# Attention kernel on one core: the slope-times-distance term of the latent heads added by TensorE behind each score matmul

## The chip, the cores and the metric

One core of one Trainium2 chip runs the whole program. The metric is the device time of one execution in microseconds. Three runs of the kernel before gave 2083.8, 2086.52 and 2086.84 us; the median is 2086.52 us.

## The reference, cut to what matters

The reference is three transformer layers for one sequence of 512 tokens at width 1024. Only the last layer's attention is touched here. It has 16 heads of dimension 64. Heads 0 to 7 of the kernel's order ("dilated" heads) use three causal windows; heads 8 to 15 ("latent" heads) attend to at most 128 keys that an indexer chose:

```
s = einsum('bqhr,bqkr->bhqk', q_lat, c_sel) * HEAD_DIM ** -0.5
dist = t_pos - idx                        # how far back the key lies
s = s - slopes[h] * dist
s = where(idx <= t_pos, s, -inf)
p = softmax(s)
```

The slopes of the latent heads are 2^-1 to 2^-8. The kernel computes all keys on and below the block diagonal and adds a large negative number where the indexer did not choose a key.

## The kernel before, in words

**Stages.** TensorE (PE) walks through 302 weight chunks (13 projections and feed-forward stages) with three one-pass matmuls per tile (lines L421 to L423: both operands split into a high and a low part in the rounded format fp32r). GpSimd splits the weights (L403, L405), SyncE's queue loads them. Between `attn_in` and `attn_out` lies the attention of the last layer, which is the part at issue.

**The attention in pairs.** Sixteen heads are done in eight pairs p = 0 to 7; pairs 0 to 3 are the dilated heads, pairs 4 to 7 the latent ones. Head a = 0 of a pair has its 64 query and key dimensions on partitions 0 to 63 of the tile `T2`, head a = 1 on partitions 64 to 127. The 512 queries are four blocks j = 0 to 3 of 128, and block j needs keys 0 to 128(j+1), so a head has 128 + 256 + 384 + 512 = 1280 score columns.

**PE's order** (written out by hand). `scores(p)` makes eight plain float32 matmuls (L863), one for each head and block in the order `SCORE_ORDER`, which alternates the heads: (0,3), (1,3), (0,1), (1,2), (0,2), (1,1), (0,0), (1,0). A float32 matmul leaves two records in the trace (two passes over its columns). The two heads' results lie in different banks but for (0,1) and (1,1), which share one: (1,1) waits for the semaphore `att_half` that (0,1) raises. `turn(p, pieces)` transposes the probabilities (L882), `values(p)` multiplies them with the values (L896). PE's loop over p is: turn(p, pieces 0 and 1); scores(p+2); turn(p, pieces 2, 3 and 4); values(p). `scores(p+2)` waits for `att_z` of both heads of pair p+1, that is, until VectorE has read their scores from PSUM.

**VectorE's order.** `bias(g)` for head g makes what is to be added to the scores. For g < 8 it is one instruction (L1453, 128x512). For g >= 8 it is four (L1457), one for each block: distance (`DL`) times minus the slope plus the indexer's mask (`SC`), into `BI`. `logits(g)` (L1470, four instructions) adds `BI` to the scores in PSUM, writes the result to SBUF and takes the row maximum; L1474 negates the maxima. `normalise(g)` (L1479, L1481) divides by the row sums. `pair_low(k)` (L1486) makes the low part of a pair's output. The loop over p is: bias(2p+4), bias(2p+5), pair_low(p-1), normalise(2p+2), logits(2p+4), normalise(2p+3), logits(2p+5). From p = 2 the two bias calls are those of latent heads; the last ones are at p = 5.

**ScalarE's order.** `exps(2p+2)` (L1847: exponential with row sums, each with a record that reads the sum), `copy_turned(p)` (four copies L1859 and one L1861, each behind a piece of `turn`), `exps(2p+3)`, `pair_high(p)` (L1867).

**Small loads.** Before the stage `idx_in`, when PE has ended the chunks before it, ScalarE issues four DMAs (L1786 to L1789: the index weights, the distances, two small projections), then computes the square root of a norm (`root`, L1794). VectorE waits for their semaphore `small_loaded` before it splits the index weights (L1393, L1395), which PE needs behind the sixth chunk of `idx_in` (its matmuls stand as `mix<-h_hi,b_wihi`).

Of the kernel before, what the change touches and what calls it, by code (L numbers as in the profile page):

```python
# [26 lines left out]
F32 = mybir.dt.float32  # L27
F32R = mybir.dt.float32r
U8 = mybir.dt.uint8
ALU = mybir.AluOpType  # L30
# [3 lines left out]
P = 128  # L34
D = 1024
T = 512
KT = D // P
NTB = T // P
# [6 lines left out]
TRI = sum(T - P * i for i in range(NTB))  # L45
# [48 lines left out]
SLOPE_A, SLOPE_B = slopes()  # L94
# [69 lines left out]
        self.n = self.base + count * per  # L164


def build(nc, x_in, wstream, adastream, c_in, cols_in, const_in, mask_in, gatew_in, wiw_in, wuk_in, wuv_in, out):
    with ExitStack() as ctx:
        def sem(name):
            return ctx.enter_context(nc.semaphore(name))  # L170
# [1 line left out]
        def sb(name, shape, dt=F32, where=ctx):  # L172
            return where.enter_context(nc.sbuf_tensor(name, shape, dt))
# [85 lines left out]
        with ExitStack() as r:  # L259
            sb("b_over_h", [P, 2 * KT * T], F32, r)  # L260

            T2 = sb("b_t2", [P, 18, T], F32, r)
            VA = sb("b_va", [P, NTB, T], F32, r)
            SC = sb("b_score", [P, TRI], F32, r)
            DL = sb("b_dist", [P, 1024], F32, r)
            BI = sb("b_bias", [P, 4, TRI], F32, r)
            zmem = ada_raw[:].rearrange("p s n -> p (s n)")
            Z = [zmem[:, TRI * i:TRI * i + TRI] for i in range(3)] + [cact[:].rearrange("p m n -> p (m n)")[:, 0:TRI]]  # L270
            PS = sb("b_pt", [P, 2, TRI], F32, r)
            VB = work
            SB5 = M + [G[3]]
            wuk = sb("b_wuk", [P, 4, P], F32, r)
            wuv = sb("b_wuv", [P, T], F32, r)
            wi_f = BI[:, 0, 0:64]
            wi_hi = sb("b_wihi", [P, 64], F32R, r)
            wi_lo = sb("b_wilo", [P, 64], F32R, r)
            wi = sb("b_wi", [P, 32], F32, r)
            wirow = PS[0:8, 0, 0:T]  # L280
            top8 = sb("b_top8", [P, 24], F32, r)
            mx = sb("b_mx", [P, 16], F32, r)
            nmx = sb("b_nmx", [P, 16], F32, r)
            rsm = sb("b_rsm", [P, 16], F32, r)
            sm = sb("b_sm", [P, 16], F32, r)
# [38 lines left out]
        def sig(name):  # L324

            if name not in S:
                S[name] = sem(name)
            return S[name]
# [90 lines left out]
        def _(pe):  # L419
# [206 lines left out]
            for h in range(4):  # L626
# [3 lines left out]
                o = M[h]  # L630
# [218 lines left out]
            def scores(p):  # L849
                if p == 0:  # L850
                    pe.wait_ge(sig("vb_copied"), 4)
                    pe.wait_ge(gfree[3], G0["attn_out"][3])
                else:
                    if p == 4:
                        pe.wait_ge(gfree[1], G0["attn_out"][1])
                    pe.wait_ge(sig("att_z"), 2 * p)
                q0, k0 = (10, 14) if p < 4 else (6, 0)
                for a, j in SCORE_ORDER:
                    rows = slice(64 * a, 64 * a + 64)
                    b, o = PAIR_J[a][j]  # L860
                    if (a, j) == (1, 1):
                        pe.wait_ge(sig("att_half"), p + 1)
                    mm = pe.matmul(SB5[b][:, o:o + P * (j + 1)], T2[rows, q0 + p % 4, j * P:(j + 1) * P],  # L863
                                   T2[rows, k0 + p % 4, 0:P * (j + 1)], start=True, stop=True)
                    if (a, j) == (0, 1):
                        mm.then_inc(sig("att_half"), 1)
                    if j == 0:
                        mm.then_inc(sig(f"att_s{a}"), 1)
# [52 lines left out]
        def _(dve):  # L921
# [467 lines left out]
            norm(7, 6, col("g_attn", 0, 8), (96, 104), first_gain=col("final_g", 0, 8))  # L1389
            normed_x(4, col("final_g", 0, 8), bank=M[1], done=True)  # L1390

            dve.wait_ge(small_loaded, 112)
            dve.tensor_copy(wi_hi[:], wi_f[:]).then_inc(sig("wi_hi"), 1)  # L1393
            dve.wait_ge(sig("wi_hi"), 1)
            dve.tensor_tensor(wi_lo[:], wi_f[:], wi_hi[:].bitcast(F32), ALU.subtract).then_inc(sig("wi_split"), 1)  # L1395
# [1 line left out]
            def seg(j, n=None):  # L1397
                return slice(OFF_J[j], OFF_J[j] + (P * (j + 1) if n is None else n))
# [51 lines left out]
            def bias(g):  # L1450

                if g < 8:
                    dve.scalar_tensor_tensor(out=BI[:, g % 4, 0:T], in0=DL[:, 0:T], scalar=-SLOPE_A[g], in1=DL[:, T:2 * T],  # L1453
                                             op0=ALU.mult, op1=ALU.add).then_inc(sig("att_b"), 1)
                else:
                    for j in range(NTB):
                        ins = dve.scalar_tensor_tensor(out=BI[:, g % 4, seg(j)], in0=DL[:, 384 - P * j:T], scalar=-SLOPE_B[g - 8],  # L1457
                                                       in1=SC[:, seg(j)], op0=ALU.mult, op1=ALU.add)
                    ins.then_inc(sig("att_b"), 1)

            def logits(g):
                q = 4 * (g % 4)
                dve.wait_ge(sig(f"att_s{g % 2}"), g // 2 + 1)
                dve.wait_ge(sig("att_b"), g + 1)
                if g >= 4:
                    dve.wait_ge(sig("att_t"), 5 * (g // 2 - 2) + 5)
                for j in range(NTB):
                    b, o = PAIR_J[g % 2][j]
                    bi = BI[:, g % 4, 384 - P * j:T] if g < 8 else BI[:, g % 4, seg(j)]
                    ins = dve.tensor_tensor_reduce(Z[g % 4][:, seg(j)], SB5[b][:, o:o + P * (j + 1)], bi, 1.0, TAKEN, ALU.add, ALU.max,  # L1470
                                                   mx[:, q + j:q + j + 1])
                ins.then_inc(sig("att_z"), 1)
                dve.wait_ge(sig("att_z"), g + 1)
                dve.tensor_scalar(nmx[:, q:q + 4], mx[:, q:q + 4], -1.0, None, ALU.mult).then_inc(sig("att_m"), 1)  # L1474
# [19 lines left out]
            logits(2)  # L1494
            logits(3)
            for p in range(8):
                if p + 2 < 8:
                    bias(2 * p + 4)
                    bias(2 * p + 5)
                if p >= 1:  # L1500
                    pair_low(p - 1)
                for a in range(2):
                    if p + 1 < 8:
                        normalise(2 * p + 2 + a)
                    if p + 2 < 8:
                        logits(2 * p + 4 + a)
# [10 lines left out]
        def _(act):  # L1517
# [269 lines left out]
            act.dma_start(DL[:], const_in[:, CST["dist"]:CST["dist"] + 1024]).then_inc(small_loaded, 16)  # L1787
            act.dma_start(wuk[:], wuk_in).then_inc(small_loaded, 16)
            act.dma_start(wuv[:], wuv_in).then_inc(small_loaded, 16)  # L1789

            def root():
                nrm[0] += 1
# [121 lines left out]
def prepare(i):  # L1914
# [35 lines left out]
    cols[0:8, COL["gate_b"] + 1] = i["odd_gate_b"][0, 8:16]  # L1950
    c, m = constants()

    def small(w_):
        n = w_.shape[1]
        return np.ascontiguousarray(w_.reshape(8, 128, n).transpose(1, 0, 2).reshape(128, 8 * n))
# [3 lines left out]
    return {  # L1959
        "x_in": np.ascontiguousarray(i["x"][0].T.reshape(8, 128, 512).transpose(1, 0, 2)),  # L1960
        "wstream": wstream, "adastream": adastream, "c_in": np.ascontiguousarray(np.broadcast_to(crow, (128, 2, 1024))), "cols_in": cols, "const_in": c, "mask_in": m,
        "gatew_in": small(gates), "wiw_in": small(wi),
        "wuk_in": np.ascontiguousarray(i["w_uk_2"][0].reshape(4, 128, 128).transpose(2, 0, 1)),
        "wuv_in": np.ascontiguousarray(i["w_uv_2"][0].transpose(1, 0, 2).reshape(128, 512)),
    }
# [13 lines left out]
```

## Time and profile before

| what | us |
|---|---|
| median of three runs | 2086.52 |
| the profiled execution, its own time | 2092.76 |
| its span from first to last instruction | 2090.7 |
| PE busy in the span | 1973.9 |
| VectorE (DVE) busy | 1072.5 |
| ScalarE (ACT) busy | 448.9 |
| GpSimd (POOL) busy | 1197.3 |
| mean granted TensorE clock | 0.969 |

The profiled execution is one run; its own time lies 6.2 us above the median of the three. The span leaves out 2.1 us of that execution's time, which lie before its first and behind its last instruction. A busy time counts only instructions that do work; waits are not counted. PE's ends are modelled: successive PE records overlap, so that the distance between two starts says more than a duration.

### The profile page before, as it was taken

The numbers are of one execution on the slowest core, as the hardware profiler recorded it, in microseconds if no ns is written. First come the engines' busy times: TensorE is split into PE (matmuls) and PEld (weight loads), VectorE is DVE, ScalarE is ACT, GpSimd is POOL, SyncE is SP. The second block draws the span as 40 slices with busy tenths as digits, with TensorE's granted clock in tenths as the row PEclk, the third lists the DMA queues.
The fourth block names the chain that finished last, engine by engine and source line by source line (L and its number), as shares of the span: only waits on it lengthen the run. The fifth ranks groups of instructions, "written<-read, shape, count | busy, mean of one in ns | idle before, by whom it ended". The sixth has DMA issues, their size and how long they took to land.

```text
span 2090.7 us, 25307 instructions
## 1 busy us (share of the span) xinstructions
PE 1973.9 (94%) x8738; PEld 1580.3 (76%) x8738; DVE 1072.5 (51%) x1631; ACT 448.9 (21%) x773; POOL 1197.3 (57%) x907
## 2 busy tenths in 40 slices
PE   6997887999999999998999999999998799999998
PEld 5786764888888887764788888887776588888886
DVE  4557633665554734456676555223876663223222
ACT  3300033221111013143121111002225621111100
POOL 2674500578887775522567888774352056666673
PEclk7998988999999999999999999999999999999999
DMA  7443200355554532211245554332121022222232
GB/s 288 170 142 121 98 4 0 101 181 190 192 200 171 210 128 81 80 47 34 86 158 199 188 193 161 108 108 87 51 71 41 1 81 91 100 94 97 101 106 75
DMA packets 67516, 242.22 MB, mean 116 GB/s; under 512 B 7642, under 2 KB 8026, under 8 KB 67458
## 3 DMA queue, kind: packets, MB, share of 16 engines
q1 hardware_dynamic: 64448, 232.81, 31.7%
q10 hardware_dynamic: 3010, 8.60, 1.1%
q8 instruction: 41, 0.67, 0.1%
q14 instruction: 17, 0.14, 0.0%
HBM read 239.28 MB, written 2.10 MB: 115 GB/s over the span
## 4 chain that ended last, share of the span: by engine, by line
PE 87%; DVE 5%; ACT 3%; DMA 2%; issue 2%; POOL 1%; SPq 0%; DVEq 0%; ACTq 0%; POOLq 0%
PE gemm L421 23%; PE gemm L423 23%; PE gemm L422 23%; DMA w_raw<-wstream 2%; PE gemm L448 1%; PE gemm L450 1%; PE gemm L449 1%; PE mix L603 1%; PE mix L421 1%; PE mix L422 1%; PE gemm L710 1%; PE mix L423 1%; PE mix L505 1%; PE gemm L724 1%; PE mix L863 1%
## 5 line engine op out<-in xcount | busy, mean ns | idle before, releaser
L405 POOL TENSOR_TENSOR w_lo<-w_raw,w_hi 128x1024 fp32r<-128x1024 f32 x302 | 748.2, 2478 | 25.2
L421 PE MATMUL gemm<-h_hi,w_hi 128*128 128x512 f32 x1616 | 635.0, 393 | 15.4 <-DVE h_lo L1030 6.0
L423 PE MATMUL gemm<-h_hi,w_lo 128*128 128x512 f32 x1616 | 631.4, 391 | 0.0
L422 PE MATMUL gemm<-h_lo,w_hi 128*128 128x512 f32 x1616 | 631.2, 391 | 0.0
L402 POOL TENSOR_TENSOR pool_gate<-pool_gate 128x1 f32<-128x1 f32 x298 | 119.4, 401 | 820.2 <-PE gemm L423 667.0
L421 PEld LDWEIGHTS gemm<-h_hi,w_hi 128*128 128x128 f32 x1616 | 305.2, 189 | 85.9 <-issue 16.1
L422 PEld LDWEIGHTS gemm<-h_lo,w_hi 128*128 128x128 f32 x1616 | 305.1, 189 | 63.5 <-issue 0.5
L423 PEld LDWEIGHTS gemm<-h_hi,w_lo 128*128 128x128 f32 x1616 | 304.7, 189 | 63.8
L403 POOL TENSOR_SCALAR w_hi<-w_raw 128x1024 fp32r<-128x1024 f32 x302 | 342.1, 1133 | 18.8 <-DMA w_raw<-wstream 18.8
L927 DVE CUSTOM_DVE_ANT_0 ada_raw<-ada_raw,c_act 128x1024 f32<-128x1024 f32 x128 | 210.4, 1654 | 168.7 <-DMA ada_raw<-adastream 168.5
L423 PE MATMUL gemm<-p_hi,w_lo 128*128 128x512 f32 x528 | 205.4, 389 | 0.0
L421 PE MATMUL gemm<-p_hi,w_hi 128*128 128x512 f32 x528 | 205.4, 389 | 0.0
L422 PE MATMUL gemm<-p_lo,w_hi 128*128 128x512 f32 x528 | 205.4, 389 | 0.0
L945 DVE SCALAR_TENSOR_TENSOR x_res<-gemm,modv,x_res 128x512 f32<-128x512 f32 x48 | 35.9, 748 | 248.8 <-PE gemm L423 248.8
L1215 DVE TENSOR_TENSOR work<-work,gemm 128x512 f32<-128x512 f32 x66 | 45.4, 688 | 176.7 <-PE gemm L423 138.9
L1523 ACT ACTIVATE sq_tile<-x_res 128x512 f32 (+1 forms) x56 | 35.2, 631 | 442.0 <-DVE x_res L945 435.1
L1217 DVE TENSOR_TENSOR p_lo<-work,p_hi 128x512 f32 x66 | 95.7, 1449 | 61.4 <-ACT p_hi L1694 61.4
L1187 DVE TENSOR_TENSOR sq_acc<-sq_acc,sq_tile 128x512 f32<-128x512 f32 x42 | 99.1, 2360 | 36.7 <-ACT sq_tile L1523 36.7
L421 PEld LDWEIGHTS gemm<-p_hi,w_hi 128*128 128x128 f32 x528 | 99.1, 188 | 20.7
L422 PEld LDWEIGHTS gemm<-p_lo,w_hi 128*128 128x128 f32 x528 | 99.1, 188 | 20.6
L423 PEld LDWEIGHTS gemm<-p_hi,w_lo 128*128 128x128 f32 x528 | 99.1, 188 | 20.4
L1688 ACT ACTIVATE work<-work 128x512 f32<-128x512 f32 x44 | 27.8, 633 | 310.4 <-DVE work L1210 310.4
(310 smaller groups left out, 2070.6 us busy)
## 6 DMA issues: line engine op xcount, KB each, us to landing
w_raw<-wstream SPq DMA_DIRECT2D x302, 512.0 KB, 3.5
ada_raw<-adastream SPq DMA_DIRECT2D x128, 512.0 KB, 4.6
a_early<-adastream SPq DMA_DIRECT2D x4, 1024.0 KB, 13.4
a_early<-adastream ACTq DMA_DIRECT2D x4, 1024.0 KB, 23.2
out<-x_res SPq DMA_DIRECT2D x8, 256.0 KB, 2.2
x_res<-x_in SPq DMA_DIRECT2D x2, 512.0 KB, 6.4
c_act<-c_in ACTq DMA_DIRECT2D x2, 512.0 KB, 15.0
x_res<-x_in ACTq DMA_DIRECT2D x2, 512.0 KB, 9.3
```

The lines of the kernel that those rows point to most:

```text
L402: pool.tensor_tensor(pgate[:], pgate[:], pgate[:], ALU.mult)
L403: pool.tensor_scalar(whi[s][:], raw[:, u % RAW, :], 1.0, 0.0, ALU.mult, ALU.add).then_inc(w_hi_done, 1)
L405: pool.tensor_tensor(wlo[s][:], raw[:, u % RAW, :], whi[s][:].bitcast(F32), ALU.subtract).then_inc(w_split, 1)
L421: pe.matmul(out_ap, w_h, r_h, start=first, stop=False)
L422: pe.matmul(out_ap, w_h, r_l, start=False, stop=False)
L423: return pe.matmul(out_ap, w_l, r_h, start=False, stop=last)
L927: dve.tensor_tensor_reduce(w, w, c, 1.0, start, ALU.mult, ALU.add, total).then_inc(ada_used, 1)
L945: dve.scalar_tensor_tensor(out=X[:, ds(m, 1), :].rearrange("p a t -> p (a t)"), in0=G[bank][:], scalar=modv[:, ds(gate + m, 1)], in1=X[:, ...
L1187: dve.tensor_tensor(sqacc[:], sqacc[:], sqt[:, m % 2, :], ALU.add).then_inc(sq_added, 1)
L1215: dve.tensor_tensor(work[:, 2 + jj, :], y, G[2 * jj + 1][:], ALU.mult).then_inc(gfree[2 * jj + 1], 1)
L1217: dve.tensor_tensor(Plo[:, ds(2 * i + jj, 1), :].rearrange("p a t -> p (a t)"), work[:, 2 + jj, :], Phi[:, ds(2 * i + jj, 1), :].rearrange ...
L1523: act.activation(sqt[:, slot, :], X[:, ds(m, 1), :].rearrange("p a t -> p (a t)"), ACT.Square).then_inc(sq_ready, 1)
```

## The change

Two constant rows for each head replace the product of slope and distance on VectorE. For query t and key s, minus slope times (t - s) is the sum of 1 times (slope * s) and t times (-slope), which is a matmul with a contraction over two rows. `SLP` holds (slope * s) and (-slope) on rows 0 and 1 of each head's 64 partitions, `QROW` holds 1 and t, and the other 62 rows are zero. Behind each score matmul of the pairs 4 to 7, PE adds their product to the same PSUM columns, in fp32r, with the same 64 partitions and the same width. VectorE makes no bias for heads 8 to 15 any more; `logits` adds the mask `SC` itself. Two DMAs (1 MB and 256 KB) bring the rows into `VA` and `T2[:, 17]`, which are not yet in use then, and two VectorE copies round them into `SLP` and `QROW`.

```diff
-            BI = sb("b_bias", [P, 4, TRI], F32, r)
+            BI = sb("b_bias", [P, 4, T], F32, r)
+            SLP = sb("b_slopes", [P, 4, T], F32R, r)
+            QROW = sb("b_qrow", [P, T], F32R, r)
...
             def scores(p):
                 if p == 0:
                     pe.wait_ge(sig("vb_copied"), 4)
+                    pe.wait_ge(sig("slopes_ready"), 2)
...
                     mm = pe.matmul(SB5[b][:, o:o + P * (j + 1)], T2[rows, q0 + p % 4, j * P:(j + 1) * P],
-                                   T2[rows, k0 + p % 4, 0:P * (j + 1)], start=True, stop=True)
+                                   T2[rows, k0 + p % 4, 0:P * (j + 1)], start=True, stop=p < 4)
+                    if p >= 4:
+                        mm = pe.matmul(SB5[b][:, o:o + P * (j + 1)], QROW[rows, j * P:(j + 1) * P], SLP[rows, p - 4, 0:P * (j + 1)],
+                                       start=False, stop=True)
                     if (a, j) == (0, 1):
                         mm.then_inc(sig("att_half"), 1)
...
-            dve.wait_ge(small_loaded, 112)
+            dve.wait_ge(small_loaded, 144)
+            dve.tensor_copy(SLP[:], VA[:]).then_inc(sig("slopes_ready"), 1)
+            dve.tensor_copy(QROW[:], T2[:, 17, :]).then_inc(sig("slopes_ready"), 1)
             dve.tensor_copy(wi_hi[:], wi_f[:]).then_inc(sig("wi_hi"), 1)
...
-                else:
-                    for j in range(NTB):
-                        ins = dve.scalar_tensor_tensor(out=BI[:, g % 4, seg(j)], in0=DL[:, 384 - P * j:T], scalar=-SLOPE_B[g - 8],
-                                                       in1=SC[:, seg(j)], op0=ALU.mult, op1=ALU.add)
-                    ins.then_inc(sig("att_b"), 1)
...
-                dve.wait_ge(sig("att_b"), g + 1)
+                if g < 8:
+                    dve.wait_ge(sig("att_b"), g + 1)
...
-                    bi = BI[:, g % 4, 384 - P * j:T] if g < 8 else BI[:, g % 4, seg(j)]
+                    bi = BI[:, g % 4, 384 - P * j:T] if g < 8 else SC[:, seg(j)]
...
             for p in range(8):
-                if p + 2 < 8:
+                if p < 2:
                     bias(2 * p + 4)
                     bias(2 * p + 5)
...
             act.dma_start(wuv[:], wuv_in).then_inc(small_loaded, 16)
+            act.dma_start(VA[:].rearrange("p a t -> p (a t)"), slope_in[:, 0:2048]).then_inc(small_loaded, 16)
+            act.dma_start(T2[:, 17, :], slope_in[:, 2048:2560]).then_inc(small_loaded, 16)
```

## Rows read from the trace of the kernel before

**Rows 1.** The page, parts 1 and 4: busy time, and the chain that ended last.
```profile
PE 1973.9 (94%) x8738; PEld 1580.3 (76%) x8738; DVE 1072.5 (51%) x1631; ACT 448.9 (21%) x773; POOL 1197.3 (57%) x907
...
PE 87%; DVE 5%; ACT 3%; DMA 2%; issue 2%; POOL 1%; SPq 0%; DVEq 0%; ACTq 0%; POOLq 0%
```

**Rows 2.** Windows, one per pair's turn: PE, PEld, DVE, ACT, POOL busy; clock; DMA.
```profile
1596.67:1607.31 10.64, 7.58 (x53) 5.19 (x53) 8.42 (x33) 7.68 (x24) 0.00 (x0) 1.00 0.00 0
1607.31:1619.29 11.98, 9.10 (x53) 6.62 (x53) 10.33 (x38) 7.54 (x23) 0.00 (x0) 0.86 0.01 2
1619.29:1629.84 10.55, 7.58 (x53) 5.16 (x53) 10.23 (x38) 7.59 (x24) 0.00 (x0) 1.00 0.00 0
1654.80:1666.10 11.30, 9.79 (x52) 5.46 (x52) 2.14 (x6) 5.42 (x14) 0.00 (x0) 0.78 0.01 2
```

**Rows 3.** Line L1457 alone: its instructions, least, median and longest in ns.
```profile
L1457 DVE SCALAR_TENSOR_TENSOR b_bias<-b_dist,b_score x32: 280/483/684, 1607.3 to 1643.1; 128x128 f32<-128x128 f32 x8, 128x256 f32<-128x256 f32 x8, 128x384 f32<-128x384 f32 x8, 128x512 f32<-128x512 f32 x8
```

**Rows 4.** Timeline of DVE, a turn of dilated, then one of latent heads.
```profile
1601.37 0.29 DVE L1470 CUSTOM_DVE_ANT_0 ada_raw<-mix,b_bias 128x128 f32<-128x128 f32 x1 [1.36 <-PE gemm L882]
...
1619.35 3.29 DVE L1457 SCALAR_TENSOR_TENSOR b_bias<-b_dist,b_score 128x128 f32<-128x128 f32 x8
...
1624.55 0.28 DVE L1470 CUSTOM_DVE_ANT_0 ada_raw<-mix,b_bias 128x128 f32<-128x128 f32 x1
...
1626.65 0.18 DVE L1479 RECIPROCAL b_rsm<-b_sm 128x4 f32<-128x4 f32 x1 [0.17 <-ACT ada_raw L1847]
```

**Rows 5.** The chain of waits in the latent turn: start, us, what.
```profile
1621.82 0.60 PE gemm L882 x4
...
1623.85 0.60 ACT b_pt L1861
1624.44 2.19 ACT ada_raw L1847 x8
...
1627.07 1.07 DVE ada_raw L1481 x3
...
1629.84 0.69 PE mix L863
```

**Rows 6.** Windows around two scores() calls, line L863 alone: PE and PEld busy, clock.
```profile
1607.31:1610.74 3.43, 3.43 (x16) 2.67 (x16) 0.67 0.00 0
1619.29:1621.75 2.46, 2.46 (x16) 1.76 (x16) 1.00 0.00 0
```

**Rows 7.** Timeline of PE: one pair's scores seen 0.4 and 0.9 us in; one indexer head.
```profile
1596.67 0.70 PE L863 MATMUL mix<-b_t 64*128 64x512 f32 x2 [1.84 <-DVE b_mx L1470]
...
1596.67 1.13 PE L863 MATMUL mix<-b_t 64*128 64x512 f32 x4 [1.84 <-DVE b_mx L1470]
...
1459.36 2.42 PE L813 MATMUL gemm<-b_t 64*128 64x128 f32 x8
```

**Rows 8.** The chain of waits: a one-pass matmul of 512 columns behind a float32 one.
```profile
1502.53 0.86 PE mix L531 x2
1503.38 0.23 PE gemm L421
```

**Rows 9.** The page, part 6, and ACT's timeline: DMAs issued ahead of `idx_in`.
```profile
a_early<-adastream ACTq DMA_DIRECT2D x4, 1024.0 KB, 23.2
...
1409.82 0.46 ACTq L1789 DMA_DIRECT2D b_wuv<-wuv_in  x1
1412.29 0.26 ACT L1794 ACTIVATE rms<-mix,cols 128x4 f32<-128x4 f32 x1 [3.08 <-PE mix L510]
```

**Rows 10.** Timelines of DVE and PE in `idx_in`, and DVE's line L1481.
```profile
1437.44 0.62 DVE L1393 CAST b_wihi<-b_bias 128x64 fp32r<-128x64 f32 x1
...
1463.72 1.27 DVE L1409 TENSOR_SCALAR b_score<-ada_raw,b_wi 128x128 f32<-128x128 f32 x4 [25.41 <-ACT ada_raw L1819]
...
1453.74 0.39 PE L421 MATMUL mix<-h_hi,b_wihi 128*8 128x512 f32 x1
...
L1481 DVE TENSOR_SCALAR ada_raw<-ada_raw,b_rsm 128x512 f32<-128x512 f32 x8 | 3.8, 480 | 0.0
```

More of the change, by code:

```diff
@@ L164, in left, with build @@
         self.n = self.base + count * per
-def build(nc, x_in, wstream, adastream, c_in, cols_in, const_in, mask_in, gatew_in, wiw_in, wuk_in, wuv_in, out):
+def build(nc, x_in, wstream, adastream, c_in, cols_in, const_in, mask_in, gatew_in, wiw_in, wuk_in, wuv_in, slope_in, out):
     with ExitStack() as ctx:
@@ L1951, in prepare @@
     c, m = constants()
+    rows = np.zeros((128, 5, 512), np.float32)
+    for h in range(8):
+        rows[64 * (h % 2), h // 2], rows[64 * (h % 2) + 1, h // 2] = SLOPE_B[h] * np.arange(512), -SLOPE_B[h]
+    rows[[0, 64], 4], rows[[1, 65], 4] = 1.0, np.arange(512)
     def small(w_):
@@ L1961, in prepare @@
         "wstream": wstream, "adastream": adastream, "c_in": np.ascontiguousarray(np.broadcast_to(crow, (128, 2, 1024))), "cols_in": cols, "const_in": c, "mask_in": m,
-        "gatew_in": small(gates), "wiw_in": small(wi),
+        "slope_in": rows.reshape(128, 2560), "gatew_in": small(gates), "wiw_in": small(wi),
         "wuk_in": np.ascontiguousarray(i["w_uk_2"][0].reshape(4, 128, 128).transpose(2, 0, 1)),
```

## The prediction

> **What bounds the kernel now.** I read the page first: PE is busy 1973.9 of 2090.7 us and carries 87% of the chain that ended last [rows 1]. So anything given to PE must be asked for its price, and anything taken from DVE for what it released. The change touches the turns of the latent pairs, and there the average says little: I cut the attention into one window per turn, from one start of scores() to the next [rows 2]. The dilated turn takes 10.64 us with DVE busy 8.42, the latent one 10.55 us with DVE busy 10.23. DVE looks like the bound of the latent turn, but the dilated turn, with 1.8 us less of DVE work, is no shorter. That is the first sign that DVE only fills a gap that another chain leaves.
>
> The timelines say which. In the latent turn, which starts at 1619.29, DVE makes the biases (3.29 us), then pair_low and normalise, and starts logits at 1624.55, 5.26 us into the turn, without idling. In the dilated turn it has idled 1.36 us before the same step, for the transposes on PE, and starts it 4.70 us into the turn. In both it must then wait for ScalarE's exponentials; in the latent turn for 0.17 us, at 1626.65 [rows 4, 5]. The chain of waits of the latent turn passes through none of the bias: transposes behind the scores (1621.82), the last copy (1623.85), the exponentials (2.19 us), normalise and logits of the second head, and the next scores at 1629.84 [rows 5]. So the turn is: scores on PE (2.46 us [rows 6]), then 8.1 us of transposes, copies, exponentials, normalise and logits, one behind the other. The scores stand at full length in this chain, because PE issues the transposes behind them.
>
> **The change part by part.**
>
> Removed: 32 bias instructions on DVE, 8 in each of four turns [rows 3], 3.29 us a turn, 13.2 us in all [rows 4]. I cost this at nothing. What hides it is the chain PE, ScalarE. Without it DVE comes to logits 3.29 us earlier and must wait there until the transposes end, 4.70 us into the turn as in the dilated one; logits starts 0.56 us earlier than now, and then normalise still waits for the exponentials, which end where they end. The bound from above is 3.29 us a turn, if the wait of 0.17 us were an illusion of the records; it is nearest to zero, since two turns with such different DVE work differ by 0.09 us. Reading the mask in place of the bias is the same shape and costs the same.
>
> Added on PE: eight one-pass matmuls behind the eight score matmuls of a pair, four pairs. A one-pass matmul of 512 columns takes 0.23 us from start to start, also right behind a float32 one, so changing the format costs nothing visible [rows 8]. One head has 1280 columns: 1280/512 x 0.23 = 0.575 us. Do the two heads of a pair share this time? Now they do: 0.4 us into a pair's scores two records of 512 columns have started, 0.9 us in it is four, and a pair ends in 2.46 us where one indexer head, the same 1280 float32 columns on one half of the rows, takes 2.42 us [rows 6, 7]. The heads run side by side, each on its 64 rows, though the code lists both passes of one head's matmul before those of the other. The added matmuls have the same rows and widths and alternate in the same way, so I take 0.575 us a pair. The ends are 0 (they fill pauses, of which 2.46 us for 2.42 us leaves few) and 1.15 us (the added ones of the two heads don't overlap); the row nearest is that of the score matmuls themselves.
>
> The first of the four, scores(4), now takes 3.43 us because the granted clock there is 0.67 on average, part of it at 1.2 GHz [rows 6]. Up to its start nothing changes, so I expect the low clock in the same place, and its added matmuls at twice the time: 1.15 us. Sum on PE's chain: 3 x 0.575 + 1.15 = 2.9 us. After the last pair's scores the same delay runs on to attn_out, since values and transposes of the pair wait behind them.
>
> The semaphore att_half is now raised behind the added matmul of (0,1). Behind the waiting (1,1) stand (0,0) and (1,0) of the same pair and all transposes. But head 1 has its own added matmuls of 512 and 384 columns before it, and these are longer than head 0's of 512 and 256, so the wait grows by nothing.
>
> The Trainium skill, page "TensorE: Matmul & The Clock Gate", section "What overlaps and what doesn't", speaks against that: matmuls start and end in program order, "strict FIFO, no reordering". By that rule a head's matmul could not begin before the first head's last pass has begun, and each added matmul would move it further back; the trace of before disagrees already, as four records have started after 0.9 us.
>
> Ahead of idx_in: two more DMA issues on ScalarE's queue. The four that stand there take 0.33 to 0.63 us each, the last starts at 1409.82; two more of 0.5 us end near 1411.3, and root, next in the queue, waits for PE until 1412.29 in any case [rows 9]. Cost nothing, with 1 us to spare; if they took over 1 us each, what is more would go to the norm and so to the chain. The 1.25 MB must have landed when DVE comes to the split of the index weights at 1437.44. The large DMAs on this queue at the kernel's start landed in 23.2 us with three others of their size under way [rows 9], which gives 1434. The copies: 2048 + 512 columns, between 0.48 us (L1481) and 0.62 us (the cast at 1437.44) for each 512, so 2.4 to 3.1 us. The split would end near 1441.5, PE needs it at 1453.74 and DVE's next work comes at 1463.72 after 25.41 us of idling [rows 10]. Hidden with 12 us to spare; SyncE's and GpSimd's queues are not passed. The new wait of scores(0) for slopes_ready has long been met.
>
> **Sum.** 0 on DVE + 2.9 on PE + 0 ahead of idx_in. The profiled execution would go from 2092.8 to 2095.7 us. It is 6.2 us above the median of the runs shown, so I put the sum on the median: 2086.5 + 2.9 = 2089.4 us. That is 0.14%, less than the 0.2% (4.2 us) that a measurement of this kernel can tell from no change.
>
> **The rivals.**
>
> *The second head waits.* PE must hold the added matmul of head 0, behind two passes, before it can start head 1. If what it can hold is one matmul less than that, the heads run one after the other. A pair's scores then last at least 2 x 2.42 = 4.84 us with the added ones beside the other head's passes, at most 4.84 + 1.15 = 5.99 us. Against 2.46 us now that is 2.4 to 3.5 us for each of four pairs, 9.5 to 14.1 us; I take 11.5: 2098.0 us. Slower is decided from 1 us a pair on. For it: the trace shows overlap for alternating matmuls alone, not for two of a head in a row. Against it: the overlap reaches over two passes already. Partly so, with 5 to 8 us, belongs here.
>
> *DVE was the bound.* If logits of the first head, 0.56 us earlier, moves ScalarE's exponentials of the next turn and these the copies, the latent turns shrink. At the most each loses its 3.29 us and gains 0.575 us: 4 x 2.7 = 10.9 us, 2075.6 us. For it: DVE is busy 10.23 of 10.55 us. Against it: the dilated turn, and PE and ScalarE with 7.6 us busy in a fixed order [rows 2].
>
> *The clock.* The turn at 1607.31 has 0.86 of the clock and lasts 1.43 us longer than its neighbours; the stretch from 1654.80 has 0.78, which on 11.30 us is some 2.5 us [rows 2]. PE works more in these turns and may be granted more: without both lows the sum is 2.9 - 0.6 - 1.4 - 2.5 = -1.6, 2084.9 us. Or the shifted work meets one low more: 1.4 to 2.5 us, 2091.4 us at the middle.
>
> *It doesn't do what it says*: the biases are removed beyond doubt; only the load ahead of idx_in could undo it, if it lands after 1449 or so; then each further us costs one.
>
> **How the numbers follow.** Forecast, its own range 2087.5 to 2091.5: 0.60. The second head waits, wholly or partly: 0.16. The clock, better 0.08, worse 0.10. DVE was the bound: 0.04. The late load: 0.02. The range starts at 2084.9, rounded to 2084.5 (better clock), and ends at 2097.0, which takes in the upper bound of the added matmuls (5.75 us), the worse clock and the lower half of the waiting head, and leaves out its upper half and the gain on DVE. Faster by over 0.2% (below 2082.3): the 0.04. Slower by over 0.2% (above 2090.7): 0.16 + 0.06 of the clock + 0.02 + 0.04 of the forecast's upper edge = 0.28. Within: 0.68.
>
> **What would show it.** Right: scores of pairs 5 to 7 last 3.0 us in place of 2.46, the turns 11.1 us, and DVE idles some 3 us more in each, most of it before logits for the transposes. Wrong: the scores records of a pair stretched to 4.8 us or more, with four 512-column records no longer started within 0.9 us (the second head waits); turns shorter than 10.5 us (DVE was the bound); ScalarE's root starting behind 1412.3, or PE idle before the index weights (the loads).

## The result, and the profile after

The changed kernel took 2092.11 us (median of 19 runs, 2089.19 to 2098.14), the kernel before 2087.84 us (median of 19 runs beside them). The ratio is 1.0024, with a 95% interval of 1.0017 to 1.0031, that is 3.5 to 6.5 us more. The time lies in the wide range given (2084.5 to 2097.0), but 0.6 us above the forecast's own range of 2087.5 to 2091.5. The ratio is a little over the 0.2% that I had set as the bound of "no change" (a chance of 0.28), and its interval reaches from just under that bound to 0.31%. It reaches 0.07% to either side, so that such a comparison tells more than the 0.2% I had thought.

The page of the changed kernel answers to [rows 1]. PE's busy time is as before, and so is its share of the chain (87%); VectorE has 6.9 us less to do over the whole program.

```profile
PE 1974.2 (94%) x8770; PEld 1581.5 (76%) x8770; DVE 1065.6 (51%) x1601; ACT 448.9 (21%) x773; POOL 1197.6 (57%) x907
```

A stretch that can be compared runs from the first score matmul of pair 3 to the first matmul of `attn_out`. Everything behind it takes 424.6 us in both profiles, and ahead of it the executions differ by several us from one to the next, change or none. I call it the stretch. The windows answer to [rows 2]: first the whole stretch, before and after, then the turns of the changed kernel. (PE, PEld, DVE, ACT, POOL busy; then the granted clock.)

```profile
1596.67:1666.10 69.43, 51.40 (x324) 34.30 (x324) 53.69 (x192) 46.17 (x130) 0.00 (x0) 0.93 0.00 1
```

```profile
1592.37:1665.47 73.10, 55.01 (x356) 37.89 (x356) 41.01 (x160) 46.12 (x130) 0.00 (x0) 0.91 0.00 1
...
1592.37:1603.00 10.63, 7.57 (x52) 5.18 (x53) 8.40 (x33) 7.67 (x24) 0.00 (x0) 1.00 0.00 0
1603.00:1615.64 12.64, 9.67 (x61) 7.34 (x61) 7.03 (x30) 7.50 (x23) 0.00 (x0) 0.86 0.01 2
1615.64:1626.70 11.06, 8.10 (x60) 5.73 (x60) 7.11 (x30) 7.57 (x23) 0.00 (x0) 1.00 0.00 0
1626.70:1637.78 11.08, 8.11 (x61) 5.75 (x61) 7.12 (x30) 7.60 (x24) 0.00 (x0) 1.00 0.01 1
1637.78:1665.47 27.69, 21.55 (x124) 13.89 (x124) 11.35 (x42) 15.77 (x41) 0.00 (x0) 0.82 0.00 1
```

The stretch grew from 69.43 to 73.10 us. VectorE's work in it fell from 53.69 to 41.01 us, and no turn became shorter for it. The last dilated turn is unchanged at 10.63 us. The latent ones stand at 12.64, 11.06 and 11.08 us against 11.98, 10.55 and 10.55 [rows 2], and from the last pair's scores to `attn_out` it is 27.69 us, where before it was:

```profile
1640.38:1666.10 25.72, 19.56 (x116) 12.18 (x116) 14.48 (x50) 15.78 (x42) 0.00 (x0) 0.87 0.01 2
```

So 0.66 + 0.51 + 0.53 + 1.97 = 3.67 us. The windows around the four scores() calls answer to [rows 6]; the clock is the number behind the bracketed counts and times.

```profile
1603.00:1607.46 4.46, 4.46 (x24) 3.85 (x25) 2.01 (x7) 0.87 (x2) 0.00 (x0) 0.64 0.00 0
1615.64:1618.62 2.98, 2.98 (x24) 2.34 (x24) 2.10 (x7) 0.96 (x2) 0.00 (x0) 1.00 0.00 0
...
1637.78:1642.39 4.61, 4.61 (x25) 3.65 (x25) 2.09 (x7) 0.96 (x2) 0.00 (x0) 0.63 0.00 0
```

At full clock the scores of a pair went from 2.46 to 2.98 us. The first and the last call had the low clock (0.64 and 0.63 on average). The first one did before, too [rows 6]; the last one did not.

PE's timeline of the second latent pair, seen 1.0 us in, answers to [rows 7], and VectorE's of that turn to [rows 4]:

```profile
1615.64 1.13 PE L866 MATMUL mix<-b_t 64*128 64x512 f32 x4 [1.85 <-DVE b_mx L1474]
1616.20 0.80 PE L869 MATMUL mix<-b_slopes,b_qrow 64*128 64x512 f32 x2
```

```profile
1620.83 0.29 DVE L1474 CUSTOM_DVE_ANT_0 ada_raw<-mix,b_score 128x128 f32<-128x128 f32 x1 [3.06 <-PE gemm L888]
...
1623.52 0.18 DVE L1483 RECIPROCAL b_rsm<-b_sm 128x4 f32<-128x4 f32 x1 [0.75 <-ACT ada_raw L1853]
```

Four score records and both added ones (L869) are there within 0.9 us: the heads still run side by side. VectorE is ready for logits 2.1 us into the turn, 3.1 us earlier than before, and idles 3.06 us until the transposes (L888) and later 0.75 us until the exponentials. The 3.29 us of [rows 4] became 3.6 us more of waiting (3.06 + 0.75 in place of 0.17). The chain of waits has the added matmuls in it and is otherwise that of [rows 5]:

```profile
1616.77 0.23 PE mix L869 x2
...
1618.69 0.60 PE gemm L888 x4
...
1621.32 2.18 ACT ada_raw L1853 x8
...
1623.94 1.07 DVE ada_raw L1485 x3
...
1626.70 0.69 PE mix L866
```

Ahead of `idx_in`, against [rows 9, 10]: ScalarE's timeline, then VectorE's and PE's.

```profile
1406.41 0.45 ACTq L1795 DMA_DIRECT2D b_t<-slope_in  x1
1407.96 0.26 ACT L1800 ACTIVATE rms<-mix,cols 128x4 f32<-128x4 f32 x1 [3.03 <-PE mix L512]
```

```profile
1433.16 1.65 DVE L1399 CAST b_slopes<-b_va 128x2048 fp32r<-128x2048 f32 x1
1434.73 0.41 DVE L1400 CAST b_qrow<-b_t 128x512 fp32r<-128x512 f32 x1
...
1459.44 1.27 DVE L1417 TENSOR_SCALAR b_score<-ada_raw,b_wi 128x128 f32<-128x128 f32 x4 [23.17 <-ACT ada_raw L1825]
```

```profile
1449.46 0.39 PE L423 MATMUL mix<-h_hi,b_wihi 128*8 128x512 f32 x1
```

The two new DMAs are issued by 1406.86 (the line shows the second of them), 1.1 us before root. VectorE made the copies in 1.65 + 0.41 us without waiting for the data and idled 23.17 us afterwards. From root to the index weights' first matmul it is 41.50 us, 41.45 before [rows 9, 10].

### The profile page after: what moved, and what is told of

It is laid out like the page before. It is cut to its first block, busy times and chain, and to the rows that moved or that the text cites. A ratio compares the mean times of both kernels' runs of the same rounds, so it can differ in the third digit from the quotient of the medians.

```text
span 2090.1 us, 25343 instructions
## 1 busy us (share of the span) xinstructions
PE 1974.2 (94%) x8770; PEld 1581.5 (76%) x8770; DVE 1065.6 (51%) x1601; ACT 448.9 (21%) x773; POOL 1197.6 (57%) x907
## 4 chain that ended last, share of the span: by engine, by line
PE 87%; DVE 5%; ACT 3%; DMA 2%; issue 2%; POOL 1%; SPq 0%; DVEq 0%; ACTq 0%; POOLq 0%
PE gemm L423 23%; PE gemm L424 23%; PE gemm L425 23%; DMA w_raw<-wstream 2%; PE gemm L450 1%; PE gemm L452 1%; PE gemm L451 1%; PE mix L605 1%; PE mix L423 1%; PE mix L424 1%; PE gemm L712 1%; PE mix L425 1%; PE mix L507 1%; PE mix L866 1%; PE gemm L726 1%
## 5 line engine op out<-in xcount | busy, mean ns | idle before, releaser
L933 DVE CUSTOM_DVE_ANT_0 ada_raw<-ada_raw,c_act 128x1024 f32<-128x1024 f32 x128 | 216.1, 1699 | 163.8 <-DMA ada_raw<-adastream 163.7
```

The source lines that it names most:

```text
L933: dve.tensor_tensor_reduce(w, w, c, 1.0, start, ALU.mult, ALU.add, total).then_inc(ada_used, 1)
```

## The experiments

Each kernel is compared with runs of the kernel before on the same chip. What it is written against (the changed kernel, or the one before) stands with it.

**1. No added matmuls** (changed kernel; the distance is added by nobody).

```diff
-                    if p >= 4:
-                        mm = pe.matmul(SB5[b][...], QROW[rows, ...], SLP[rows, p - 4, ...], start=False, stop=True)
```

> The changed kernel without the added matmuls: VectorE makes no bias for the latent heads and nobody adds the distance; the loads and the two copies ahead of idx_in stay. Measure: the stretch from the first score matmul of pair 3 to the first matmul of attn_out, 69.4 us before and 73.1 us after the change in the profiles. Theory (VectorE's bias work was wholly hidden, the added matmuls are the whole loss): scores of a latent pair 2.46 us again, the stretch 69.4 us or less by at most 0.2, time that of the kernel before (2087.8 us). Rival 1 (taking the bias away gave something back, and the added matmuls cost more than they show): the stretch is 66 us or less, the time 3 us or more below before. Rival 2 (the loads and copies ahead of idx_in cost something): time above before although the stretch is 69.4 us.

Measured: 2090.4 us, ratio to the kernel before 1.0002 (0.9991 to 1.0013). The stretch, and the scores of the second latent pair:

```profile
1597.51:1666.94 69.43, 51.36 (x325) 34.28 (x325) 41.02 (x160) 46.12 (x130) 0.00 (x0) 0.93 0.00 1
1620.18:1622.64 2.46, 2.46 (x16) 1.76 (x17) 2.10 (x7) 0.96 (x3) 0.00 (x0) 1.00 0.00 0
```

69.43 us to the hundredth, as in the kernel before, with 12.7 us less on VectorE. Rival 1 is out: taking the bias away gave nothing. Rival 2 is out as well, as loads and copies are in this kernel and the time is that of the kernel before.

**2. Added matmuls and biases both.** The 32 bias instructions are back on VectorE, into a tile that is read by nobody.

```diff
+                else:
+                    dve.wait_ge(sig("att_b"), g)
+                    for j in range(NTB):
+                        ins = dve.scalar_tensor_tensor(out=BX[:, seg(j)], in0=DL[:, 384 - P * j:T], scalar=-SLOPE_B[g - 8], in1=SC[:, seg(j)], ...)
+                    ins.then_inc(sig("att_b"), 1)
...
-                if p < 2:
+                if p + 2 < 8:
                     bias(2 * p + 4)
```

> The changed kernel with the added matmuls and also the 32 bias instructions on VectorE (their result is written and used by nobody, a wait on its own semaphore stands before each group). Theory: the bias work is hidden here as it was before; the latent turns last 11.1 us as after the change, the time is that of the changed kernel within 1 us (2092 us). With 0.17 us of VectorE's slack plus 0.52 us of longer scores it fits by 0.1 us or less, so up to 0.3 us a turn may show. Rival 1: each turn is 1 us or more longer than after the change, the time 2096 us or more.

Measured: 2096.46 us, ratio 1.0030 (1.0018 to 1.0042). The stretch and one turn:

```profile
1591.74:1664.79 73.05, 54.94 (x356) 38.15 (x356) 54.06 (x192) 46.11 (x130) 0.00 (x0) 0.91 0.00 1
1615.01:1626.08 11.07, 8.11 (x60) 5.74 (x61) 10.32 (x38) 7.58 (x24) 0.00 (x0) 1.00 0.00 0
```

73.05 us, and the turn of 11.07 us is that after the change, with VectorE busy 10.32 us in place of 7.11. The median lies 4 us above what I expected, and the rival had 2096 us or more; but on this chip the kernel before took 2089.51 us, the interval holds the changed kernel's ratio, and the rival's turns, 1 us longer each, are not there. The bias is hidden with the added matmuls as without.

**3. Each added matmul twice** (the distance counts double).

```diff
                     if p >= 4:
-                        mm = pe.matmul(...)
+                        for last in (False, True):
+                            mm = pe.matmul(..., start=False, stop=last)
```

> The changed kernel with each added matmul issued twice (the distance counts double). Theory: scores of a pair at full clock go from 2.46 (none) and 2.98 us (one) to 3.5 us, each turn 0.52 us longer than after the change, one of the four at the lower clock twice that; the stretch 73.1 + 2.6 = 75.7 us, the time 2.6 us above the changed kernel (2094.7 us). Rival (PE can hold one added matmul beside two passes but not two, so the second head waits): scores of a pair 4.8 us or more, the time 7 us or more above the changed kernel. Rival 2 (the clock took much of the loss by chance): the stretch moves by anything from 1 to 5 us, by where the low clock falls.

Measured: 2095.19 us, ratio 1.0029 (1.0017 to 1.0040). The stretch, and the scores of a pair that ran at full clock:

```profile
1593.00:1668.87 75.87, 58.06 (x389) 41.85 (x389) 40.92 (x160) 46.25 (x130) 0.00 (x0) 0.91 0.00 1
1630.39:1634.06 3.67, 3.67 (x32) 3.02 (x32) 2.10 (x7) 0.97 (x3) 0.00 (x0) 1.00 0.00 0
```

At full clock the scores take 3.67 us: the first added matmul of each block cost a pair 0.52 us, the second 0.69. The heads still overlap. That the stretch of 75.87 us meets the 75.7 of the theory is in part luck, as the second rival of the expectation would have it: the granted clock was 0.68 in the scores of pairs 4, 5 and 7, one pair more than after the change, and from the last pair's scores on it is 26.72 us at a clock of 0.87, where it was 27.69 us at 0.82. The times (ratio 1.0029 against 1.0024) are too coarse to show the further 2.8 us, as their intervals overlap.

**4. The added matmuls behind piece 4 of turn.** They leave the scores() call and stand where PE waits 0.78 us for ScalarE's last copy.

```diff
                 turn(p, (2, 3, 4))
+                if 4 <= p + 2 < 8:
+                    distances(p + 2)      # the eight added matmuls, then att_s0 and att_s1
                 values(p)
```

> The changed kernel with the eight added matmuls moved from behind each score matmul to behind the transposes of piece 4, where PE waits 0.78 us for ScalarE's last copy. Theory (only their place in the chain costs time): scores of a latent pair 2.46 us, the turns 10.5 to 10.7 us, the stretch 69.4 us, the time that of the kernel before (2087.8 us) though VectorE makes no bias. Rival: VectorE's logits, which now wait for the added matmuls 5.2 us into the turn, come later than the exponentials and the turn grows by 0.3 us or more: stretch 70.6 us or more.

Measured: 2089.19 us, ratio 1.0002 (0.9994 to 1.0011).

```profile
1592.48:1661.90 69.42, 54.51 (x356) 37.15 (x356) 41.01 (x160) 46.18 (x130) 0.00 (x0) 0.93 0.00 1
```

In three banks two blocks lie side by side, and here both are started before anything is added, so that the score product of the block written first is missing from its sum. The Trainium skill, page "PSUM — Partial Sum Buffer", section "The four PSUM rules", says that a start flag clears the written marks of the whole bank and that the next matmul without one overwrites. No time here shows the marks. The following kernel leaves the flag out for the second block of a bank:

```diff
-                                   T2[rows, k0 + p % 4, 0:P * (j + 1)], start=True, stop=True)
+                                   T2[rows, k0 + p % 4, 0:P * (j + 1)], start=(a, j) not in ((0, 0), (1, 0), (1, 1)) or p < 4, ...)
```

> As the added matmuls behind the transposes of piece 4, but the second score matmul in a bank that holds two blocks doesn't start an accumulation, so that the added matmuls find what they add to. Theory: the same times as in that run, stretch 69.4 us, time that of the kernel before. Rival: a flag changes the time: stretch off by 0.3 us or more.

Measured: 2086.99 us, ratio 0.9994 (0.9985 to 1.0004). The stretch, and the second latent turn:

```profile
1589.64:1659.06 69.42, 54.53 (x356) 37.18 (x356) 41.03 (x160) 46.16 (x129) 0.00 (x0) 0.93 0.00 1
1612.24:1622.78 10.54, 8.35 (x60) 5.86 (x61) 7.12 (x30) 7.59 (x24) 0.00 (x0) 1.00 0.00 0
```

The same matmuls as after the change, the same work on VectorE, and the stretch is back at 69.42 us: what cost time was their place in the chain. The further low of the clock, which the last pair's scores met after the change, is gone with it. VectorE has 41.0 us to do in place of 53.7, and the time is that of the kernel before.

**5. The heads in runs of three** (changed kernel, all pairs).

```diff
-SCORE_ORDER = [(0, 3), (1, 3), (0, 1), (1, 2), (0, 2), (1, 1), (0, 0), (1, 0)]
+SCORE_ORDER = [(0, 1), (0, 3), (0, 2), (1, 1), (1, 3), (1, 2), (0, 0), (1, 0)]
```

> The changed kernel with another order of the score matmuls in all eight pairs: (0,1), (0,3), (0,2), (1,1), (1,3), (1,2), (0,0), (1,0), three of head 0 and then three of head 1, each latent one with its added matmul behind it. It asks how far PE looks past a head's waiting matmuls, which is what the rival of the prediction hung on. Theory (each head's rows have a queue of limited length, which was long enough for one float32 matmul and one added one, and the doubling of the added ones did not fill it): the second head starts late, when most of the first's three are through; scores of a dilated pair near 4.3 us, of a latent pair near 5.3 us, each turn longer by the difference: stretch 73.1 + 0.9 to 1.8 a dilated pair's turn, 2 a latent one's, some 83 us in all, time 12 us or more above the changed kernel. Rival (the queue is long): the heads run side by side, scores of a latent pair 3.0 to 3.3 us, stretch 73 to 75 us.

Measured: 2104.38 us, ratio 1.0072 (1.0058 to 1.0087). Windows of PE alone (busy; clock): scores of a dilated and of a latent pair, and the stretch. Then PE's timeline in short windows: two lines of the dilated scores, the others of the latent ones.

```profile
1584.66:1587.77 3.11, 3.11 (x18) 1.00 0.02 7
1607.12:1613.22 6.10, 6.10 (x25) 0.72 0.00 0
1595.84:1684.05 88.21, 71.10 (x356) 0.81 0.00 1
```

```profile
1584.66 0.70 PE L866 MATMUL mix<-b_t 64*128 64x256 f32 x2
...
1585.19 0.70 PE L866 MATMUL mix<-b_t 64*128 64x512 f32 x2
...
1607.12 0.67 PE L866 MATMUL mix<-b_t 64*128 64x256 f32 x2 [1.93 <-DVE b_mx L1474]
1607.44 0.47 PE L869 MATMUL mix<-b_slopes,b_qrow 64*128 64x256 f32 x1
...
1608.20 0.79 PE L869 MATMUL mix<-b_slopes,b_qrow 64*128 64x512 f32 x1
1608.61 0.48 PE L866 MATMUL mix<-b_t 64*128 64x256 f32 x1
```

I had overlooked a semaphore in this order. Head 1 now begins with (1,1), which waits for `att_half`, and that is raised by (0,1), the first matmul of head 0 (by its added one in a latent pair). In a dilated pair this wait explains the whole delay: (0,1) ends at 1585.36, and (1,1) starts at 1585.41, 0.05 us later (its first record is the second one of the line at 1585.19, which also holds the first pass of (0,3)), although the second pass of (0,3) and all of (0,2) stand ahead of it and have not started. The call lost 0.65 us (3.11 for 2.46 us). In a latent pair the added matmul of (0,1) ends at 1607.91, but (1,1) starts only at 1608.61, 1.49 us after head 0's first record and still at full clock. Of these, 0.79 us are the wait for the semaphore. The other 0.70 us are not: there head 1 does start late, behind three matmuls of head 0 with their added ones, as a limited queue would have it. That it is a queue is argued, not shown; an order of the same kind without the semaphore was not run.

The latent calls took 6.10 us in three pairs, at a clock of 0.72, and 8.24 us in the last at 0.52, so I can't say what they take at full clock. The stretch of 88.21 us is 5 us beyond my figure, and the clock (0.81 over it, 0.91 after the change) has a large part in that.

**6. Turn before scores.** In the first of two, the kernel before has all pieces of turn(p) ahead of scores(p+2); in the second, the changed kernel.

```diff
-                turn(p, (0, 1))
+                turn(p, (0, 1, 2, 3, 4))
                 if p + 2 < 8:
                     scores(p + 2)
-                turn(p, (2, 3, 4))
                 values(p)
```

> The kernel before (biases on VectorE) with PE's loop in another order: all five pieces of turn(p), then scores(p+2), then values(p). So the scores leave the chain transposes, copies, exponentials. Theory: with that chain shorter VectorE becomes the bound of the latent turns: it is busy 10.23 us in each, so they last 10.2 to 10.5 us, while the dilated turns shrink to 9 us or so. Stretch 67 to 69 us (69.4 now), time 1 to 3 us below the kernel before. Rival (ScalarE and the semaphores set 10.5 us in any order): stretch 69 us or more.

> The changed kernel with the same order of PE's loop. Theory: now the work that the change takes from VectorE counts: its latent turns hold 7 us of VectorE's and 7.6 us of ScalarE's work, and last 8.5 to 9.5 us; the stretch is 63 to 66 us, 3 us or more shorter than that of the kernel before in the same order, and the time 4 to 7 us below the kernel before. Rival (the added matmuls and the waits for the exponentials keep the turn): turns of 10.3 us or more, no better than the kernel before in the same order.

Measured: 2087.86 us, ratio 1.0001 (0.9993 to 1.0010), and 2092.17 us, ratio 1.0018 (1.0009 to 1.0026). For kernels in another order I take the longer stretch from the first score matmul of pair 1 to `attn_out`: 94.97 us before, 98.64 us after the change. The long stretch and a latent turn of each:

```profile
1566.57:1661.10 94.53, 73.39 (x450) 50.14 (x449) 64.97 (x239) 57.93 (x162) 10.71 (x9) 0.95 0.07 23
1607.30:1617.65 10.35, 7.55 (x54) 4.94 (x53) 10.21 (x38) 7.59 (x22) 0.00 (x0) 0.99 0.00 1
```

```profile
1568.28:1666.71 98.43, 77.01 (x482) 52.62 (x481) 52.31 (x207) 57.83 (x162) 10.73 (x9) 0.93 0.06 22
1632.39:1643.25 10.86, 8.06 (x62) 5.52 (x61) 7.02 (x29) 7.59 (x22) 0.00 (x0) 1.00 0.01 2
...
DVE ada_raw L1473 <- PE mix L869: 16.4, 4, 5.3
ACT h_hi L1872 <- PE gemm L902: 14.2, 5, 3.8
```

Both theories fell, and the turns are those of the rivals. In the first kernel the last dilated turn takes 10.32 us (I had 9) and the latent one 10.35, so that VectorE's 2 us more of work do not show. In the second the last dilated turn takes 10.33 us and the latent one 10.86 at full clock, with 3.2 us less on VectorE: taking the bias away gave nothing, and the added matmuls cost their 0.5 us again. VectorE waits 16.4 us for the scores and ScalarE 14.2 us for the values (the wait list of the second kernel): the scores now wait for the transposes, the values for the scores, and ScalarE's next exponentials stand behind the output of the values. One chain was exchanged for another of nearly the same length.

**7. The second head's exponentials early.** ScalarE waits 2.2 us for the transposes behind the scores, and the second head's exponentials take 2.18 us, are ready to run, and stand behind that wait. Three kernels move them ahead of it: the kernel before, the changed kernel, and the changed one with the added matmuls between pieces 3 and 4 of turn.

```diff
                 if p + 1 < 8:
                     exps(2 * p + 2)
-                copy_turned(p)
+                if p >= 1:
+                    pair_high(p - 1)
+                copy_turned(p, (0, 1))
                 if p + 1 < 8:
                     exps(2 * p + 3)
-                pair_high(p)
+                copy_turned(p, (2, 3, 4))
...
-                if p >= 1:
-                    pair_low(p - 1)
-                for a in range(2):
-                    if p + 1 < 8:
-                        normalise(2 * p + 2 + a)
-                    if p + 2 < 8:
-                        logits(2 * p + 4 + a)
+                normalise(2 * p + 2); pair_low(p - 1); normalise(2 * p + 3)
+                logits(2 * p + 4); logits(2 * p + 5)
```

> The kernel before with another order on ScalarE and VectorE. ScalarE: exps(2p+2), pair_high(p-1), two copies, exps(2p+3), three copies; so the second head's exponentials (2.18 us) run where ScalarE waited 2.2 us for the scores on PE, and leave the chain. VectorE: normalise of both heads, then logits of both. Measure here: from the first score matmul of pair 1 to the first matmul of attn_out, 95.0 us before, 98.6 us after the change. Theory (VectorE's bias was hidden only by that chain): once the chain is shorter the 3.29 us stand in the turn: VectorE's work of a latent turn adds up to 10.2 us and more, so the latent turns stay at 10.2 to 10.9 us, the dilated ones (1.3 us of bias) fall to 9.0 to 9.6 us. Stretch 91 to 95 us, time 0 to 4 us below the kernel before. Rival (PE and ScalarE set the turns in this order too): latent turns as short as dilated ones, 9.0 to 9.6 us, stretch 88 us or less.

> The changed kernel, added matmuls behind each score matmul, with that same order on ScalarE and VectorE. Theory: VectorE's latent turn is 3.3 us shorter and PE's scores 0.52 us longer; turns of 9.0 to 9.9 us, latent ones no longer than dilated ones by more than 0.6 us; stretch 88 to 91 us, shorter than that of the kernel before in the same order, time 5 to 8 us below the kernel before. Rival (the added matmuls cost as much as the bias there): latent turns 10.2 us or more.

> The same order, with the added matmuls between the transposes of pieces 3 and 4, where PE waits for ScalarE's copy. Theory: latent turns 9.0 to 9.5 us, 0.3 to 0.5 us shorter than with the added matmuls among the scores; stretch 86 to 89 us, time 6 to 10 us below the kernel before, faster than both kernels. Rival (they are no longer on the chain in this order): the same within 0.2 us a turn as with them among the scores.

Measured, in this order: 2085.74 us, ratio 0.9986 (0.9977 to 0.9995); 2083.34 us, ratio 0.9973 (0.9964 to 0.9983); 2082.14 us, ratio 0.9969 (0.9957 to 0.9981). The long stretch and latent turns of each:

```profile
1566.61:1659.17 92.56, 74.32 (x450) 50.44 (x449) 65.39 (x239) 56.88 (x162) 10.75 (x9) 0.93 0.07 23
1600.87:1611.86 10.99, 9.18 (x53) 5.82 (x52) 10.85 (x40) 8.11 (x25) 0.00 (x0) 0.84 0.01 2
1611.86:1621.37 9.51, 7.59 (x54) 5.16 (x53) 9.37 (x35) 6.63 (x21) 0.00 (x0) 1.00 0.00 0
```

```profile
1564.31:1653.11 88.80, 73.39 (x482) 51.62 (x481) 53.20 (x207) 56.87 (x162) 10.75 (x9) 0.96 0.07 24
1607.89:1617.22 9.33, 8.03 (x61) 5.73 (x60) 7.17 (x29) 7.49 (x23) 0.00 (x0) 1.00 0.00 0
```

```profile
1566.86:1655.63 88.77, 74.50 (x481) 52.09 (x480) 53.21 (x207) 56.86 (x162) 10.73 (x9) 0.96 0.07 24
1610.46:1619.79 9.33, 8.32 (x62) 5.87 (x61) 7.17 (x29) 7.49 (x23) 0.00 (x0) 1.00 0.00 0
```

Both changed kernels beat the kernel before and the change as it was made: 88.80 and 88.77 us in place of 94.97 and 98.64. Of the 6.2 us against the kernel before, 1.4 come with the clock: pair 4's turn, 11.98 us there, has no low in either. Their turns are 9.33 us whether the added matmuls are among the scores or not, so that in this order they are no longer on the chain (the rival of the last expectation, and my own figure of 0.3 to 0.5 us was wrong). The kernel before in the same order has VectorE busy 9.37 of 9.51 us in its turn at full clock: the bias is now the bound, but only by 0.18 us; I had expected 10.2 us or more. That its stretch of 92.56 us lies in my range of 91 to 95 is luck: some 3 of the 3.8 us by which it is longer than that of the changed kernel come with the clock (0.84 and 0.85 in two turns). What makes the clock fall there and not in the other two I have not shown, nor, then, how much of the 2.4 us between the medians the bias is worth.

**8. The changed kernel again.**

> The changed kernel once more, unchanged. In its profile one stretch of half clock (3.4 us) more than before lies in the last pair's scores; it took 1.5 of the 3.7 us by which the attention grew. Theory (the work sets where the clock falls, since the low 1.2 us into the scores of pair 4 came at the same place in every profile): it comes again, in the scores or transposes of one of the pairs 5 to 7, and the stretch from the first score matmul of pair 3 to attn_out is 72.8 to 73.4 us. Rival (a chance of that one execution): no further low, the stretch is 71.3 to 71.8 us.

Measured: 2093.58 us, ratio 1.0019 (1.0007 to 1.0031). The stretch, and the scores of pair 6:

```profile
1598.30:1671.36 73.06, 54.95 (x357) 38.16 (x357) 41.04 (x160) 46.10 (x129) 0.00 (x0) 0.91 0.00 1
1632.63:1636.92 4.29, 4.29 (x24) 3.65 (x24) 2.10 (x7) 0.97 (x3) 0.00 (x0) 0.67 0.00 0
```

73.06 us. The further low came again, this time in pair 6 instead of pair 7, at nearly the same price: pair 6's turn took 12.63 us, pair 5's 11.06.

## Why the prediction was right or wrong

**VectorE's bias, cost nothing: right, and shown.** With the biases and without, the stretch is 69.43 us if nothing is added on PE (experiment 1), and 73.05 and 73.10 us if it is (experiment 2). The cover that I named, the chain of PE and ScalarE, is what hides it: shortened by 1.2 us in experiment 7, it no longer quite does. The rival "DVE was the bound" is out.

**The added matmuls, 0.575 us a pair: right in kind, 0.52 us.** The two heads share the time. The rival "the second head waits" did not come about, and the doubling of experiment 3 did not bring it about; in experiment 5, with three matmuls of one head in a row, 0.70 us of such a wait show beside that for `att_half`. The rule of the Trainium skill that I set against it (page "TensorE: Matmul & The Clock Gate", section "What overlaps and what doesn't": matmuls start in the order of the program) does not hold in these traces. After the change head 0's added matmul stands ahead of head 1's score matmul in the program, and both score matmuls are under way 0.5 us before the first added one starts (1615.64 and 1616.20). The wait for `att_half`, which I had put at nothing, leaves no mark either: the call grew by less than the added columns take.

**scores(4) at the low clock, 1.15 us: right in part.** The call itself grew by 1.03 us (3.43 to 4.46), but the turn only by 0.66. The turn's granted clock is 0.86 before and after, so its time at 1.2 GHz hardly grew. I had doubled the added work and not asked what the rest of the turn gets back: what the added matmuls take of the low, the transposes behind them no longer do.

**Sum 3 x 0.575 + 1.15 = 2.9 us: it failed at its last term.** I took the clock of the later pairs to be full, and gave one low more a chance of 0.10. It came in all three executions with a profile whose scores carry one added matmul each in this order (after the change, experiments 2 and 8), in pair 6 or 7, and cost about 1.5 us: 1.97 us after the change where 0.575 was put. The parts are now 0.66 + 0.51 + 0.53 + 1.97 = 3.67 us, 0.18%, and two comparisons of runs gave 0.24% and 0.19%, with intervals that hold it; on which side of 0.2% the change lies they leave open. The rival "the clock", in its worse form, had 2091.4 us and is what happened. Part of the remaining distance is the base: I had added the sum to the median of three runs, 2086.52 us, and that of the 19 was 2087.84, which would have made it 2090.7.

**Ahead of idx_in, nothing: right.** The DMAs were issued 1.1 us before root could start, the data were there when VectorE came, and the copies took 2.06 us, less than the 2.4 to 3.1 us that I had worked out from other instructions.

**What stays open.** Why the clock falls once more. It goes with the added matmuls among the scores in this order of the work. None of the four profiles with turns of 10.5 us has it, and two of these are of experiment 4, which has the same added matmuls in another place. The changed kernels of experiment 7 carry them too and have fewer lows, and the kernel before has one low more in their order than in its own.

## What to carry to other kernels

An engine that is busy 97% of a loop's turn is not its bound until something shows that a turn with less of its work is shorter; here the neighbouring turn with 1.8 us less was as long, and 12.7 us of work could be taken away for nothing. Work that is moved to the engine on the chain costs nearly its full time at one place (0.52 us a turn) and nothing at another a few instructions later, so look first for where that engine waits. And work taken off a hidden engine can become worth something only when the chain gets shorter; here that was 0.18 us a turn at full clock, and what the clock added I can't ascribe. The larger gain, 1.0 us a turn with the biases still there, came from the order alone: from moving the instructions that were ready to run and stood behind a wait of their own length.

## What the runs showed of the hardware that I had not expected

The low clock comes at a place that the work sets. In the kernel before, after the change and in experiments 1, 2, 4 and 8 the scores of pair 4 meet it at the same point: they take 3.42 to 3.49 us where nothing is added and 4.46 to 4.49 us with one added matmul for each. The executions had drifted apart by up to 9 us by then (the stretch begins at 1589.64 us in one of them and at 1598.30 in another). With the added matmuls among the scores one low more comes, in pair 6 or 7. With the same matmuls behind the transposes (experiment 4) it does not, and in the changed kernels of experiment 7 the one in pair 4 is gone too.

A head's matmuls start although matmuls of the other head stand ahead of them in the program and still wait. With one second pass and one added matmul ahead, both heads' first records lie in the first 0.9 us and the call grew by 0.52 us; with two added ones it grew by a further 0.69. With three matmuls and their added ones ahead the other head came 1.49 us late, of which 0.79 us are its wait for a semaphore (experiment 5).

One VectorE cast of 128x2048 took 1.65 us, 0.41 us for each 512 columns, as much as the single one of 512.
